# Values of a head pair multiplied by turns, and the levels' score products by turns from the two halves of the rows

## The chip, the cores and the metric

The kernel runs on one core of a Trainium2 chip. The metric is the device time of one execution in microseconds (us), as the median of several runs. TensorE (PE in the profile) multiplies, VectorE (DVE), ScalarE (ACT) and GpSimd (POOL) do the elementwise work, and SyncE (SP) issues the transfers from device memory. Each engine works through its own list of instructions in order. Semaphores make one engine wait for another.

## The reference

Two blocks run one after the other on 256 tokens of width 1024 (272 with the 16 meta tokens in the first block). The first block has two layers, each a mixer and a feed-forward part; the second has gated linear attention (GLA) beside a convolution, then a feed-forward part and a gate. The change touches two places:

```
# first block, first layer: attention, 16 heads, causal
s = jnp.einsum('bqhd,bkhd->bhqk', qb, kb).astype(jnp.float32) * scale
p = jax.nn.softmax(s, axis=-1).astype(vb.dtype)
outs.append(jnp.einsum('bhqk,bkhd->bqhd', p, vb))     # 64 value columns for each head
return o @ w_o
...
# second block: gated linear attention, 4 heads of 64 key and 128 value columns
scores = jnp.einsum('bhtd,bhsd,bhtsd->bhts', qc, kc, decay)
o_intra = jnp.einsum('bhts,bhsv->bhtv', scores, vc)
```

The kernel computes the GLA scores without chunks, level by level: one product of the plain queries and keys for the diagonal, and one for each power of two of the distance.

## The kernel before

All activations lie transposed, with the features on the 128 partitions. A large weight matrix comes in units of some 1 MB through two slots. Each unit is split into a high part (ACT, `high`) and a low part (DVE, POOL, `low`), and every product is three matmuls (lines 436 to 438). The order on each engine is written out by hand.

**Attention.** Tokens are cut into three tiles of 96, 96 and 80. The loop over `s` in the block of TensorE is software-pipelined. At step s, PE does `head_scores(s + 1)`, `head_values(s - 3)` and `head_transposes(s - 2)`. At the steps from 15 on it also does chunks of the output projection (`out_chunks`, six matmuls for each chunk of 128 features). Each fp32 matmul of the program leaves two records in the trace.

- `head_scores(g)` (lines 614 and 616) writes banks 0 to 3 by turns. It waits for the exponentials of head g - 2.
- `head_values(g)` (line 628) multiplies the 64 value columns of head g by its transposed probabilities, with 272, 176 and 80 columns moving. Even heads write partitions 0 to 63 of a bank, odd heads 64 to 127; so the two heads of a pair use two halves of the columns of the PE array. It waits for the copies of the transposed probabilities of head g.
- `head_transposes(g)` (line 644) writes banks 4 and 5.

ACT at its step s does: the copy of the transposed probabilities of head s - 3 (line 1047), the exponentials of head s (line 1056), and at odd s from 5 on the high part of a pair's output (line 1061), which waits for the values of the pair's second head. DVE at its step s does: the row maxima and their negative of head s (lines 1475, 1477), the copies of bank 5 of head s - 3 (lines 1487, 1488), the reciprocals of head s - 1 (line 1495), and at odd s the low part of the pair's output (line 1501), which waits for the high part. POOL scales the probabilities (line 1776) into three buffers. At step 16 ACT first makes the high part of the next weight unit (line 876).

**GLA levels.** `level(l)` (line 764) does eight matmuls with 64 rows of the array each (four for the level `FAR`): first all four from partitions 0 to 63, which write bank 6, then all four from partitions 64 to 127, which write bank 7. There are nine levels, each placed between or within units of the input projections. DVE makes a level's operands (`level_operands`, lines 1557 to 1565), and after its products keeps them by a mask (`level_kept`, line 1579 for all but the last). A level's products wait for its operands and for the masks of the level before; DVE's masks wait for the level's last product.

Of the kernel before, what the change touches and what calls it, by code (L numbers as in the profile page):

```python
# [48 lines left out]
T1 = META + SEQ  # L49
# [4 lines left out]
NH, NOPE, ROPE, VD = 16, 64, 32, 64  # L54
# [8 lines left out]
PTOFF = [0, T1, T1 + 176]  # L63
# [6 lines left out]
FAR, DIAGONAL = 7, 8  # L70
# [117 lines left out]
def program(nc, dram, marks, final):  # L188
    ctx = ExitStack()
    with ctx:  # L190
        def sb(name, shape, dt=F32, stack=None):
            return (stack or ctx).enter_context(nc.sbuf_tensor(name, shape, dt))
# [6 lines left out]
        def done(name, i=None):  # L199


            engine, n, loop = marks.get(name, ("scalar", 1, None))
            stride = marks.get(("stride", engine, loop), 1)
            if final and name not in marks:
                raise KeyError(name)
            if isinstance(i, tuple):
                i, n = i[0], n - i[1] * stride
            return step_sems[engine], n if i is None else i * stride + n
# [42 lines left out]
        V = sb("v_tokens", [96, 3, D], stack=mla)  # L251
# [17 lines left out]
        PT = sb("probs_t", [96, 2, 528], stack=att)  # L269
# [20 lines left out]
        bank = [ctx.enter_context(nc.psum_tensor(f"bank{b}", [P, 512], F32)) for b in range(8)]  # L290
# [125 lines left out]
        def _(pe):  # L416
            S = Steps("tensor", step_sems["tensor"], marks)

            def parts_ready(n, i=None):

                at = n + 1 if i is None else 2 * i + (n + 1)
                pe.wait_ge(high_parts, at)
                pe.wait_ge(low_parts_v, at)
                if pool_share(n):
                    pe.wait_ge(low_parts_g, at)
# [14 lines left out]
            def weights(n, j):  # L440
                return wh[n % 2][:, j * P:(j + 1) * P], wl[n % 2][:, j * P:(j + 1) * P]
# [175 lines left out]
                                            skip_group_check=True)  # L617
                last.then_inc(*S.step(f"scores {g}"))

            def head_values(g):  # L620
                pair, half = g // 2, g % 2
                pe.wait_ge(*done(f"transposed a {g}"))
                pe.wait_ge(*done(f"transposed b {g}"))
                if half == 0 and pair >= 2:
                    pe.wait_ge(*done(f"att out {pair - 2} low"))
                o = bank[6 + pair % 2][64 * half:64 * half + 64, :]
                for c, (k0, nk) in enumerate(QT):
                    last = nc.tensor.matmul(o[:, k0:T1], V[0:nk, c, g * VD:(g + 1) * VD],  # L628
                                            PT[0:nk, g % 2, PTOFF[c]:PTOFF[c] + T1 - k0],
                                            start=c == 0, stop=c == 2)  # L630
                last.then_inc(*S.step(f"values {g}"))

            def head_transposes(g):
                pe.wait_ge(*done(f"probs {g}"))
# [27 lines left out]
            def out_chunks(chunks):  # L662


                n = FIRST_UNIT["wo"]
                for k in chunks:
                    if k == 0:
                        parts_ready(n)
                        pe.wait_ge(*done(f"exp {NH - 2}"))
                    att_ready(k)  # L670
                    for b in range(2):
                        hi, lo = weights(n, k * 2 + b)
                        last = three(bank[BLOCKS[UNITS[n]["first"] + b]["bank"]][:, 0:T1], hi, lo,
                                     uh[:, k, 0:T1], ul[:, k, 0:T1], k == 0, k == DC - 1)
                        if k == DC - 1:
                            last.then_inc(products, 1)

            def att_ready(k):
                pe.wait_ge(*done(f"att out {k} high"))
                pe.wait_ge(*done(f"att out {k} low"))  # L680

            for s in range(2, NH + 3):
                if s + 1 < NH:
                    head_scores(s + 1)
                if s >= 3:
                    head_values(s - 3)
                if s >= NH - 1:
                    out_chunks(((0, 1), (2, 3), (4, 5), (6,))[s - NH + 1])
                if s < NH + 2:
                    head_transposes(s - 2)  # L690
            out_chunks((7,))
# [17 lines left out]
            for half in range(2):  # L709
                for t, (t0, nt_) in enumerate(TT):  # L710
                    b = first + half * len(TT) + t
                    bank_free(b)
                    for g in range(2 * half, 2 * half + 2):
                        out = bank[BLOCKS[b]["bank"]][0:nt_, (g % 2) * 256:(g % 2) * 256 + 256]
                        for k in range(2):
                            if t == 0:
# [4 lines left out]
                            last = nc.tensor.matmul(out, ul[:, 2 * g + k, toks], wh[n % 2][:, at],  # L721
                                                    start=False, stop=k == 1)
# [4 lines left out]
            for c in range(DC):  # L727
                half, g = c // 4, c // 2

                pe.wait_ge(freed["a"], BLOCKS[first + half * len(TT) + len(TT) - 1]["freed"])  # L730
                b = first + 2 * len(TT) + c
                bank_free(b)
                for t, (t0, nt_) in enumerate(TT):
                    last = nc.tensor.matmul(bank[BLOCKS[b]["bank"]][:, t0:T1], pz[0:nt_, t, c * P:(c + 1) * P],  # L734
                                            wm[0:nt_, g, WIN_AT[t]:WIN_AT[t] + T1 - t0],
                                            start=t == 0, stop=t == len(TT) - 1)
# [9 lines left out]
            def level(l):  # L746

                if l == DIAGONAL:
                    pe.wait_ge(freed["v"], BLOCKS[FIRST_BLOCK["gin_k"] + 1]["freed"])
                    pe.wait_ge(*done("gate inputs"))  # L750
                else:
                    pe.wait_ge(*done(f"level {l} q"))
                    pe.wait_ge(*done(f"level {l} k"))
                    pe.wait_ge(*done(f"level {LEVEL_BEFORE[l]} kept 1"))
                qs, ks = (gq, gk) if l == DIAGONAL else (ql, kl)
                for half in range(2):
                    part = slice(64 * half, 64 * half + 64)
                    for pair in range(2):
                        for i in range(2):
                            if l == FAR and i:  # L760
                                continue
                            j = 1 if l == FAR else i
                            o = (pair if l == FAR else pair * 2 + i) * P
                            last = nc.tensor.matmul(bank[6 + half][:, o:o + P],  # L764
                                                    ks[part, pair * SEQ + i * P:pair * SEQ + (i + 1) * P],
                                                    qs[part, pair * SEQ + j * P:pair * SEQ + (j + 1) * P],
                                                    start=True, stop=True)
                last.then_inc(*S.step(f"level {l} scores"))
# [9 lines left out]
            for pair in range(2):  # L778
                last = nc.tensor.matmul(bank[6][:, pair * SEQ:(pair + 1) * SEQ], wgu[:, pair * P:(pair + 1) * P],
                                        glr[0:16, :], start=True, stop=True)  # L780
            last.then_inc(*S.step("gate logits"))

            for v in range(2):
                n = FIRST_UNIT["gin_v"] + v
                parts_ready(n)
                for t in range(2):
                    b = UNITS[n]["first"] + t
                    bank_free(b)
                    out = bank[BLOCKS[b]["bank"]][:, 0:256]
                    for k in range(DC):  # L790
# [3 lines left out]
                        last = nc.tensor.matmul(out, ul[:, k, toks], wh[n % 2][:, at], start=False, stop=k == DC - 1)  # L794
# [24 lines left out]


            level(LEVEL_ORDER[0])
            unit(FIRST_UNIT["gin_g"], T, us)
            level(LEVEL_ORDER[1])
# [1113 lines left out]
```

## Time and profile before

| | |
|---|---|
| median of 3 runs | 966.16 us (965.82 to 967.49) |
| the profiled execution's own time | 969.12 us |
| its span | 967.3 us |
| busy PE, DVE, ACT, POOL | 919.7, 686.3, 513.5, 304.7 us |
| attention loop, values of head 0 to the last output chunk | 80.9 to 128 us |
| GLA levels | 637 to 688 us |

The busy time of an engine is an average over stages with different limits. A row of the timeline gives the start, the length, the engine, the line of the kernel, and in brackets the idle time of the engine just before it with what ended it. Times of one row are from the start of the span.

### The profile page before, as it was taken

What the parts mean: (1) busy time and instruction counts of PE and PEld (TensorE: products, weight loads), DVE (VectorE), ACT (ScalarE), POOL (GpSimd) and SP (SyncE); (2) the same over time, 40 slices, a digit from 0 to 9 for tenths busy, and PEclk for the clock granted to TensorE, in tenths of its full rate; (3) what the DMA queues carried; (4) which work ended last, traced back from release to release, by engine and by line L of the source; (5) the groups of instructions that cost most, each with busy time, mean ns of one, the idle gap of its engine ahead of it and who ended that gap; (6) DMA issues with size and microseconds to landing.
All of it is one profiled execution on the core that took longest, in us unless ns stands there. A gap on an engine that the chain in (4) does not pass through costs nothing.

```text
span 967.3 us, 19946 instructions
## 1 busy us (share of the span) xinstructions
PE 919.7 (95%) x7300; PEld 893.6 (92%) x7300; DVE 686.3 (71%) x1165; ACT 513.5 (53%) x850; POOL 304.7 (31%) x215
## 2 busy tenths in 40 slices
PE   6999998999999998899999899999989999999996
PEld 6997788999998997799999899899989999999995
DVE  7756527999995225599999523879787887885666
ACT  5675655666664335756666444453346444554433
POOL 4107753000004552400000455331226243345643
PEclk9999997999999997899999999899999999999998
DMA  7451032444454451045555445243235555555431
GB/s 255 159 163 44 1 130 88 175 173 173 173 206 155 151 197 67 1 176 193 190 179 206 149 169 198 100 181 131 88 109 192 184 180 179 200 211 201 164 131 44
DMA packets 22145, 146.77 MB, mean 152 GB/s; under 512 B 2752, under 2 KB 5328, under 8 KB 6736
## 3 DMA queue, kind: packets, MB, share of 16 engines
q1 hardware_dynamic: 22096, 146.11, 42.4%
q8 instruction: 32, 0.52, 0.2%
q14 instruction: 17, 0.14, 0.0%
HBM read 143.94 MB, written 1.05 MB: 150 GB/s over the span
## 4 chain that ended last, share of the span: by engine, by line
PE 83%; DVE 11%; ACT 3%; issue 2%; DMA 0%; POOL 0%; SPq 0%; POOLq 0%; DVEq 0%; ACTq 0%
PE bank L436 24%; PE bank L437 23%; PE bank L438 23%; DVE w_low L1227 2%; PE bank L628 2%; PE bank L614 2%; PE bank L506 1%; DVE conv_out L1358 1%; DVE u_low L1236 1%; ACT w_high L876 1%; PE bank L495 1%; PE bank L734 1%; PE bank L644 1%; DVE h L1309 1%; PE bank L764 1%
## 5 line engine op out<-in xcount | busy, mean ns | idle before, releaser
L436 PE MATMUL bank<-u_high,w_high 128*128 128x256 f32 (+2 forms) x1472 | 425.6, 289 | 18.4 <-DVE u_low L1236 16.8
L437 PE MATMUL bank<-u_low,w_high 128*128 128x256 f32 (+2 forms) x1472 | 422.2, 287 | 0.0
L438 PE MATMUL bank<-u_high,w_low 128*128 128x256 f32 (+2 forms) x1472 | 420.8, 286 | 0.0
L1727 POOL TENSOR_TENSOR w_low<-raw,w_high 128x512 fp32r<-128x512 f32 (+1 forms) x73 | 199.8, 2738 | 543.5 <-ACT w_high L876 543.5
L436 PEld LDWEIGHTS bank<-u_high,w_high 128*128 128x128 f32 x1472 | 282.1, 192 | 22.6 <-issue 9.8
L437 PEld LDWEIGHTS bank<-u_low,w_high 128*128 128x128 f32 x1472 | 281.9, 192 | 0.0
L438 PEld LDWEIGHTS bank<-u_high,w_low 128*128 128x128 f32 x1472 | 281.5, 191 | 0.0
L1227 DVE TENSOR_TENSOR w_low<-raw,w_high 128x1024 fp32r<-128x1024 f32 (+5 forms) x119 | 188.8, 1586 | 128.7 <-ACT w_high L876 127.4
L876 ACT ACTIVATE w_high<-raw 128x1024 fp32r<-128x1024 f32 (+5 forms) x120 | 198.0, 1650 | 71.4 <-PE bank L438 61.2
L436 PE MATMUL bank<-x_high,w_high 128*128 128x256 f32 (+1 forms) x608 | 174.9, 288 | 8.0 <-DVE x_low L1335 4.8
L438 PE MATMUL bank<-x_high,w_low 128*128 128x256 f32 (+1 forms) x608 | 174.6, 287 | 0.0
L437 PE MATMUL bank<-x_low,w_high 128*128 128x256 f32 (+1 forms) x608 | 173.9, 286 | 0.0
L436 PEld LDWEIGHTS bank<-x_high,w_high 128*128 128x128 f32 x608 | 116.9, 192 | 9.4 <-ACT conv_out L961 3.4
L437 PEld LDWEIGHTS bank<-x_low,w_high 128*128 128x128 f32 x608 | 116.7, 192 | 0.0
L438 PEld LDWEIGHTS bank<-x_high,w_low 128*128 128x128 f32 x608 | 116.5, 192 | 0.0
L873 ACT ACTIVATE w_high<-raw 128x1024 fp32r<-128x1024 f32 (+1 forms) x66 | 65.8, 996 | 75.8 <-PE bank L438 72.7
L1358 DVE SCALAR_TENSOR_TENSOR conv_out<-conv_in,par,conv_out 128x272 f32<-128x272 f32 (+1 forms) x176 | 85.4, 525 | 6.2 <-ACT conv_out L954 0.7
L1740 POOL TENSOR_TENSOR acc<-acc,sq 128x272 f32<-128x272 f32 (+2 forms) x79 | 63.8, 808 | 76.3 <-ACT sq L892 65.5
L1222 DVE TENSOR_TENSOR w_low<-raw,w_high 128x1024 fp32r<-128x1024 f32 (+1 forms) x66 | 75.4, 1143 | 12.2 <-ACT w_high L873 9.4
L1283 DVE TENSOR_TENSOR conv_in<-bank,r_rows 128x256 f32<-128x256 f32 (+2 forms) x140 | 54.1, 427 | 14.8 <-PE bank L438 9.3
L961 ACT ACTIVATE conv_out<-conv_out 128x272 f32<-128x272 f32 (+1 forms) x44 | 18.8, 426 | 76.6 <-DVE conv_out L1358 76.6
L1236 DVE SCALAR_TENSOR_TENSOR u_low<-h,par,u_high 128x272 fp32r<-128x272 f32 (+3 forms) x56 | 52.6, 957 | 0.9 <-ACT u_high L909 0.9
(194 smaller groups left out, 924.6 us busy)
## 6 DMA issues: line engine op xcount, KB each, us to landing
raw<-w_up_dram SPq DMA_DIRECT2D x66, 1024.0 KB, 4.8
raw<-w_down_dram SPq DMA_DIRECT2D x24, 1408.0 KB, 6.1
raw<-w_gin_c_dram SPq DMA_DIRECT2D x4, 1536.0 KB, 6.3
raw<-w_wo_dram SPq DMA_DIRECT2D x4, 1024.0 KB, 5.0
raw<-w_wout_dram SPq DMA_DIRECT2D x4, 1024.0 KB, 4.8
raw<-w_pgate_dram SPq DMA_DIRECT2D x4, 1024.0 KB, 4.8
raw<-w_gin_v_dram SPq DMA_DIRECT2D x2, 1024.0 KB, 4.9
raw<-w_gin_g_dram SPq DMA_DIRECT2D x2, 1024.0 KB, 4.8
```

Of the source, the lines that this page charges most:

```text
L436: nc.tensor.matmul(out, hi, rhi, start=start, stop=False)
L437: nc.tensor.matmul(out, hi, rlo, start=False, stop=False)
L438: return nc.tensor.matmul(out, lo, rhi, start=False, stop=stop)
L873: nc.scalar.activation(wh[n % 2][:, 0:split], raw[n % 2][:, 0:split], ACT.Copy).then_inc(*S.step(first))
L876: nc.scalar.activation(wh[n % 2][:, split:cols], raw[n % 2][:, split:cols], ACT.Copy).then_inc(high_parts, 1)
L1222: nc.vector.tensor_tensor(wl[n % 2][:, 0:split], raw[n % 2][:, 0:split], wh[n % 2][:, 0:split].bitcast(F32), ALU.subtract).then_inc(*S.step())
L1227: nc.vector.tensor_tensor(wl[n % 2][:, split:cols], raw[n % 2][:, split:cols], wh[n % 2][:, split:cols].bitcast(F32), ALU.subtract).then_i ...
L1236: nc.vector.scalar_tensor_tensor(ul[:, c, 0:T], h[:, c, t0:t0 + T], pcol(gain, c), uh[:, c, 0:T].bitcast(F32), ALU.mult, ALU.subtract)\
L1283: nc.vector.tensor_tensor(out, bank[BLOCKS[b]["bank"]][:, 0:T], rows[:, 0:T], ALU.mult)\
L1358: nc.vector.scalar_tensor_tensor(cv[:, hf, 0:T], ur[:, hf, skip + tap:skip + tap + T], pcol(f"cw{l}", (tap * 2 + hf) * FC + j), cv[:, hf, ...
L1727: nc.gpsimd.tensor_tensor(wl[n % 2][:, at], raw[n % 2][:, at], wh[n % 2][:, at].bitcast(F32), ALU.subtract).then_inc(low_parts_g, pool_cou ...
L1740: nc.gpsimd.tensor_tensor(acc[:, a, 0:T], acc[:, a, 0:T], sq[:, label % 2, 0:T], ALU.add).then_inc(*step)
```

## The change

In attention, `pair_values(pair)` takes the place of `head_values(g)`. It does both heads of a pair, at even steps from 4 on, and goes over the three token tiles, with the two heads by turns within each. It waits for the copies of the pair's second head, so the first head's values come one step later than before. From step 15 on the output chunks now stand ahead of the values. In the levels, the loop over the two halves of the rows becomes the innermost one. No operation is added or taken away, and no other engine's code is changed.

```diff
-            def head_values(g):
-                pair, half = g // 2, g % 2
-                pe.wait_ge(*done(f"transposed a {g}"))
-                pe.wait_ge(*done(f"transposed b {g}"))
-                if half == 0 and pair >= 2:
+            def pair_values(pair):
+                pe.wait_ge(*done(f"transposed a {2 * pair + 1}"))
+                pe.wait_ge(*done(f"transposed b {2 * pair + 1}"))
+                if pair >= 2:
                     pe.wait_ge(*done(f"att out {pair - 2} low"))
-                o = bank[6 + pair % 2][64 * half:64 * half + 64, :]
                 for c, (k0, nk) in enumerate(QT):
-                    last = nc.tensor.matmul(o[:, k0:T1], V[0:nk, c, g * VD:(g + 1) * VD],
-                                            PT[0:nk, g % 2, PTOFF[c]:PTOFF[c] + T1 - k0],
-                                            start=c == 0, stop=c == 2)
-                last.then_inc(*S.step(f"values {g}"))
+                    for half in range(2):
+                        g = 2 * pair + half
+                        last = nc.tensor.matmul(bank[6 + pair % 2][64 * half:64 * half + 64, k0:T1],
+                                                V[0:nk, c, g * VD:(g + 1) * VD],
+                                                PT[0:nk, half, PTOFF[c]:PTOFF[c] + T1 - k0],
+                                                start=c == 0, stop=c == 2)
+                        if c == 2:
+                            last.then_inc(*S.step(f"values {g}"))
...
             for s in range(2, NH + 3):
                 if s + 1 < NH:
                     head_scores(s + 1)
-                if s >= 3:
-                    head_values(s - 3)
                 if s >= NH - 1:
                     out_chunks(((0, 1), (2, 3), (4, 5), (6,))[s - NH + 1])
+                if s >= 4 and s % 2 == 0:
+                    pair_values((s - 4) // 2)
                 if s < NH + 2:
                     head_transposes(s - 2)
...
-                for half in range(2):
-                    part = slice(64 * half, 64 * half + 64)
-                    for pair in range(2):
-                        for i in range(2):
-                            if l == FAR and i:
-                                continue
+                for pair in range(2):
+                    for i in range(2):
+                        if l == FAR and i:
+                            continue
+                        for half in range(2):
+                            part = slice(64 * half, 64 * half + 64)
```

Three places on TensorE show what moves. The first is a step in the middle of the attention loop: the last masking matmul of the scores, one head's values, and the transposes. Before:

```order
L616 MATMUL bank2<-causal_bf16,ident_bf16 80x80
L628 MATMUL bank7<-probs_t,v_tokens 64x272
L628 MATMUL bank7<-probs_t,v_tokens 64x176
L628 MATMUL bank7<-probs_t,v_tokens 64x80
L644 MATMUL bank4<-ident,probs 96x96 x2
L644 MATMUL bank4<-ident,probs 96x80
L644 MATMUL bank5<-ident,probs 96x96
```

Now, at an even step (at odd steps no values stand between the scores and the transposes):

```order
L630 MATMUL bank7<-probs_t,v_tokens 64x272 x2
L630 MATMUL bank7<-probs_t,v_tokens 64x176 x2
L630 MATMUL bank7<-probs_t,v_tokens 64x80 x2
L648 MATMUL bank4<-ident,probs 96x96 x2
L648 MATMUL bank4<-ident,probs 96x80
```

The values of two heads stand in one place, every second step. The second place is the end of the loop (from step 15), where the names with `u_` and `w_` are the output projection. Before, a step's transposes are followed at once by the next head's values:

```order
L644 MATMUL bank5<-ident,probs 80x80
L628 MATMUL bank6<-probs_t,v_tokens 64x272
L628 MATMUL bank6<-probs_t,v_tokens 64x176
L628 MATMUL bank6<-probs_t,v_tokens 64x80
L436 MATMUL bank0<-u_high,w_high1 128x272
L437 MATMUL bank0<-u_low,w_high1 128x272
```

Now the chunks come first, and the values of the pair behind them, ahead of the next transposes:

```order
L436 MATMUL bank2<-u_high,w_high1 128x272
L437 MATMUL bank2<-u_low,w_high1 128x272
L438 MATMUL bank2<-u_high,w_low1 128x272
L630 MATMUL bank6<-probs_t,v_tokens 64x272 x2
L630 MATMUL bank6<-probs_t,v_tokens 64x176 x2
L630 MATMUL bank6<-probs_t,v_tokens 64x80 x2
L648 MATMUL bank4<-ident,probs 96x96 x2
```

The values moved behind the chunks. The third place is a GLA level between two units of the input projection. Before:

```order
L438 MATMUL bank1<-u_high,w_low0 128x256
L764 MATMUL bank6<-gla_q_level,gla_k_level 128x128 x4
L764 MATMUL bank7<-gla_q_level,gla_k_level 128x128 x4
L436 MATMUL bank3<-u_high,w_high1 128x256
L437 MATMUL bank3<-u_low,w_high1 128x256
```

Now:

```order
L438 MATMUL bank1<-u_high,w_low0 128x256
L769 MATMUL bank6<-gla_q_level,gla_k_level 128x128
L769 MATMUL bank7<-gla_q_level,gla_k_level 128x128
L769 MATMUL bank6<-gla_q_level,gla_k_level 128x128
L769 MATMUL bank7<-gla_q_level,gla_k_level 128x128
...
L436 MATMUL bank3<-u_high,w_high1 128x256
```

There are eight such rows (four are shown): the same eight products now change bank, and with it the half of the rows, at each of them.

## Rows read from the trace of the kernel before

**Rows 1.** The page: busy time of each engine, its share and instructions.

```profile
PE 919.7 (95%) x7300; PEld 893.6 (92%) x7300; DVE 686.3 (71%) x1165; ACT 513.5 (53%) x850; POOL 304.7 (31%) x215
```

**Rows 2.** Windows, attention loop: busy us of PE, PEld, DVE, ACT, POOL, clock, DMA.

```profile
78.00:111.80 33.80, 33.72 (x256) 25.80 (x256) 21.09 (x89) 20.27 (x86) 26.44 (x36) 1.00 0.02 8
```

**Rows 3.** Timeline, one pair's round through the engines in the attention loop.

```profile
94.87 1.11 PE L628 MATMUL bank<-probs_t,v_tokens 96*64 96x272 f32 x6
...
95.91 0.67 PE L644 MATMUL bank<-ident,probs 96*96 96x96 f32 x6
...
96.61 0.39 ACT L1047 ACTIVATE probs_t<-bank 96x272 f32<-96x272 f32 x1 [0.96 <-PE bank L644]
...
96.91 0.33 ACT L1056 ACTIVATE probs<-bank,neg_max 96x96 f32<-96x96 f32 x1
...
98.08 0.40 ACT L1061 ACTIVATE u_high<-bank 128x272 fp32r<-128x272 f32 x1
98.51 0.44 DVE L1501 TENSOR_TENSOR u_low<-bank,u_high 128x272 fp32r<-128x272 f32 x1 [1.33 <-ACT u_high L1061]
...
98.87 0.86 DVE L1475 TENSOR_REDUCE row_max<-bank 96x1 f32<-96x96 f32 x3
...
100.10 0.23 DVE L1488 COPY probs_t<-bank 80x80 f32<-80x80 f32 x1
...
100.47 1.11 PE L628 MATMUL bank<-probs_t,v_tokens 96*64 96x272 f32 x6
```

**Rows 4.** Timeline, around the values of heads 0 and 1.

```profile
81.49 0.20 ACT L1056 ACTIVATION_READ_ACCUMULATOR probs<-bank,neg_max 80x1 f32 x1
...
82.41 0.35 PE L614 MATMUL bank<-k_heads,q_heads 96*96 96x96 f32 x2
...
83.66 0.67 PE L628 MATMUL bank<-probs_t,v_tokens 96*64 96x272 f32 x2
```

**Rows 5.** Timeline, end of the attention loop.

```profile
111.79 1.11 PE L628 MATMUL bank<-probs_t,v_tokens 96*64 96x272 f32 x6
...
112.83 0.67 PE L644 MATMUL bank<-ident,probs 96*96 96x96 f32 x6
...
115.14 0.39 PE L436 MATMUL bank<-u_high,w_high 128*128 128x272 f32 x1
...
115.29 1.93 ACT L876 ACTIVATE w_high<-raw 128x2048 fp32r<-128x2048 f32 x1
...
116.75 0.63 PE L644 MATMUL bank<-ident,probs 96*96 96x96 f32 x6
...
118.08 3.63 POOL L1776 TENSOR_SCALAR probs<-probs,row_inv 96x96 f32<-96x96 f32 x3 [1.67 <-DVE row_inv L1495]
...
125.85 1.08 PE L628 MATMUL bank<-probs_t,v_tokens 96*64 96x272 f32 x6 [0.67 <-DVE probs_t L1488]
...
127.99 0.36 PE L436 MATMUL bank<-u_high,w_high 128*128 128x272 f32 x1
```

**Rows 6.** Timeline of PE in one GLA level, the whole and narrow windows of it.

```profile
644.58 1.71 PE L764 MATMUL bank<-gla_q_level,gla_k_level 64*128 64x128 f32 x16
...
644.79 0.49 PE L764 MATMUL bank<-gla_q_level,gla_k_level 64*128 64x128 f32 x3
...
645.13 0.60 PE L764 MATMUL bank<-gla_q_level,gla_k_level 64*128 64x128 f32 x6
...
646.02 0.27 PE L764 MATMUL bank<-gla_q_level,gla_k_level 64*128 64x128 f32 x1
646.22 0.39 PE L436 MATMUL bank<-u_high,w_high 128*128 128x256 f32 x1
```

**Rows 7.** Timeline of DVE, the three masks that wait for a level's products.

```profile
646.33 1.38 DVE L1579 COPY_PREDICATED gla_s_diag<-level_masks,bank 128x512 f32<-128x512 int32 x2 [1.21 <-PE bank L764]
...
657.35 1.40 DVE L1579 COPY_PREDICATED gla_s_diag<-level_masks,bank 128x512 f32<-128x512 int32 x2 [0.36 <-PE bank L764]
...
669.44 1.40 DVE L1579 COPY_PREDICATED gla_s_diag<-level_masks,bank 128x512 f32<-128x512 int32 x2 [0.82 <-PE bank L764]
```

## The prediction

> **What bounds the kernel now.** I read the page first: PE is busy for 919.7 of 967.3 us [rows 1], so what shortens PE's list can shorten the whole, but only in a stretch where nothing else ends last. So I looked at the two stretches that the change touches. In the attention loop the window shows PE busy for 33.72 of 33.80 us at the full clock, with POOL at 26.44, DVE at 21.09 and ACT at 20.27 [rows 2]. That looks like a stretch that only PE bounds. The timeline says more. I follow one pair's round from engine to engine [rows 3]. The values of a pair's second head start at 94.87 and last 1.04 until the transposes at 95.91, which end at 96.58. ACT copies (96.61), does its exponentials (96.91), then the pair's high part (98.08). DVE, which has sat idle for 1.33 us, makes the low part (98.51) and only then the next row maxima (98.87) and the copy of bank 5, which ends at 100.33. The next second head's values need that copy, and start at 100.47. The round is 5.60 us, and PE's own work of two steps is 5.60 us too. Two limits stand side by side, and the change shortens only one of them.
>
> In the GLA levels I read PE's and DVE's timelines. One level is 16 records from 644.58 to 646.22, 1.64 us [rows 6]. DVE waits for a level's products three times in all, by 1.21, 0.36 and 0.82 us [rows 7]; after all other levels the products are long there when DVE comes to mask them.
>
> **Do two halves of the array run side by side?** For halves of the rows the level's own rows answer. Three records of one half take 0.49 us and one takes 0.27, so one half steps at 0.11 us [rows 6]. Around the change of halves six records start and end within 0.60 us [rows 6], where a single line of them would have four (0.27 + 3 x 0.11). So the second half's records run beside the last ones of the first. By turns, eight records of each half run beside each other from the start. The second half begins about one step late (0.11), the first record is 0.10 longer, then seven steps of 0.11, and 0.20 from the last start to the next unit as now [rows 6]: 0.11 + 0.10 + 0.77 + 0.20 = 1.18 to 1.20 instead of 1.64, so 0.44 us less for each level. The bounds are 0 (no more overlap than now) and 0.55 (no late start).
>
> For halves of the columns (the values) no row of this trace has two such matmuls next to each other. Let d be what a pair's burst takes over one head's 1.04. If they run beside each other as the row halves do, d is one late start, 0.11. If they don't, d is a second head's streaming: 0.11 us for a record of 128 columns [rows 6] makes 0.92 for 2 x (272 + 176 + 80) columns. So d lies between 0 and 0.92, and I take 0.11, because two disjoint halves of one array are what the level rows show.
>
> The Trainium skill, TensorE: Matmul & The Clock Gate, section on packing small matmuls, would have matmuls strictly in order of start and end, and weight loads pulled beside running matmuls only where the row groups differ. The two heads of a pair use the same rows, so by that rule they would take about the serial time, which is the first rival below. The same section gives three column tiles a measured gain of 2.38 times, and by its span model a tile more costs some 4 ns, which would make d almost nothing. The six records within 0.60 us speak against its strict order of starts.
>
> **Attention, step by step.** (a) At step 3 the values of head 0 go. The scores of head 5 (82.41) could come some 1.1 us earlier (the burst of 1.04 and about 0.1 for the change into it, as the first record of a level shows [rows 6]), but they wait for the exponentials of head 3, which end at 81.69 [rows 4]. So they start at about 81.75, take 1.25 as now (82.41 to 83.66), and the first pair starts at 83.0 instead of 83.66: -0.65. (b) From here each pair starts one round after the other. The round through ACT and DVE has the pair's burst in it and nothing else of what changes, so it becomes 5.60 + d. PE's own work falls to 5.60 - 1.04 - 0.1 + d, about 4.6: the former overlap of two limits ends, and PE gets an idle gap of about 1 us ahead of each pair's values. Five rounds lie between the first pair and the one at 111.79: +5d. This is where most of the freed PE time goes. (c) The end of the loop. Now each head's values wait out the copy of the transposes just ahead (0.67 at 125.85 [rows 5]), four times. Afterwards the chunks (1.6 us for two, 115.14 to 116.75 [rows 5]) stand in that place and hide it. From the transposes at 112.83 by PE's own list the next pair could start at 112.83 + 0.50 + 1.5 + 0.47 + 1.6 = 116.9. But ACT makes a weight unit's high part from 115.29 to 117.22 and copies only then (0.39), so it starts at 117.7. Then 1.04 + d for it, 0.5 for transposes, 1.5 for chunks: transposes of head 15 at 120.75. Their probabilities come from POOL, whose row of 3.63 us starts at 118.08 [rows 5]; it is released by a copy that now comes some 1.8 us earlier, so it ends by 119.9 and stays hidden. The last pair starts 1.3 later, at 122.1, and the last chunk follows as now 2.14 after it (125.85 to 127.99 [rows 5]), at 124.25 instead of 127.99: -3.7, with 3d for three bursts on the way. In sum the loop ends -4.35 + 8d later, at d = 0.11 it is -3.5 us. What follows moves with it as one piece.
>
> **Levels.** The diagonal and the first level are each 0.44 shorter, and DVE's wait of 1.21 gives back 0.88. From there DVE is the one that is late, and level 1's products start when its operands are there. The wait of 0.36 ahead of the third mask goes altogether, as PE is 0.44 further ahead. Then three levels on PE, and the wait of 0.82 goes altogether too. 0.88 + 0.36 + 0.82 = 2.06 us. After 669.44 DVE no longer waits for a level, so the rest of the levels' PE time (9 x 0.44 less that) buys nothing. The bounds are 0 and 2.39, the sum of the three waits.
>
> **Sum.** -3.5 - 2.05 = -5.55 us. The profiled execution's own time is 969.12, span 967.3; it lies 0.3% over the median, and I take the difference off the median: 966.16 - 5.55 = 960.6.
>
> **Rivals.**
> - *The columns' halves run one after the other* (d = 0.92). For it: no row shows otherwise. Against it: the row halves do run beside each other. Attention +3.0, levels -2.05: +0.95, 967.1.
> - *Each change of half costs a drain.* This is the one on the other side. Entering a level costs 0.10 on its first record [rows 6]; if each of five turns within a pair's burst cost that as well as the serial time, d = 1.4, attention +6.9, in all +4.8, 971.0. It decides from d = 0.8 on, where loss and gain are even. Against it: the change of halves within a level costs nothing now. The Trainium skill, TensorEngine Tiling (Array Packing), key properties, has a drain for a change of the tiling mode, not of the tile; the trace agrees for halves of the rows.
> - *PE alone bounds the loop*, and my round through ACT and DVE has slack. Then each of five rounds falls by 1.14 - d = 1.03 instead of growing by d: 5.7 us more gained, 954.9. Against it: DVE's idle 1.33 us sits in the round, and its copy ends just 0.14 ahead of the values.
> - *Part of the gain is swallowed*: d near 0.3 and half of the levels' 2.05. -4.35 + 2.4 - 1.0 = -3, 963.2. DVE is nearly full around the levels, which speaks for it.
>
> **Numbers.** Mine 0.66, serial columns 0.15, a drain at each turn 0.05, PE alone 0.06, partly swallowed 0.08. A difference under 0.2% (1.9 us) is about what a measurement of this kernel can't tell from no change. Mine, PE alone and partly swallowed are faster: 0.80, less a little for their edges; serial columns is mostly within 0.2%; its edge and the drain are slower. Mine alone lies within 959 to 962.6 (d from 0.05 to 0.2, levels 1.5 to 2.4). The range reaches down half a microsecond and up to the serial case: 958.4 to 967.2.
>
> **What would show it.** After the change a pair's values should be one burst of 12 records in about 1.15 us at eight places, with starts in between closer than 0.07 us; about 2 us would mean serial. The pairs' bursts should stand 5.7 us apart, with PE idle about 1 us ahead of each, ended by DVE's copy (line 1488's operation); 4.6 us apart would make PE alone the bound. The last chunk should start 3 to 4 us earlier. A level should take 1.2 us, and the three waits of DVE should be near nothing but for 0.3 at the first. The prediction is wrong above all if d is far from 0.11, since it counts eight times.

## The result and the profile after

The changed kernel takes 961.3 us in the median of four runs (960.62 to 961.49), beside 966.83 for the kernel before in the same comparison (four runs, 965.82 to 968.22). The ratio is 0.9935, with a 95% interval of 0.9922 to 0.9949: 5.5 us faster. The forecast was 960.6, a gain of 5.55, in a range of 958.4 to 967.2.

The page answers to [rows 1]: PE's busy time fell by 12.4 us, the median time by 5.5. (The two profiled executions lie 7.7 us apart, 967.3 against 959.6 in their spans, since that of the kernel before was a long one.)

```profile
span 959.6 us, 19938 instructions
PE 907.3 (95%) x7300; PEld 883.8 (92%) x7300; DVE 685.2 (71%) x1165; ACT 512.4 (53%) x850; POOL 304.8 (32%) x215
```

The window over the attention loop (busy us of PE, PEld, DVE, ACT, POOL with their instructions, then clock and DMA) shows where the rest stayed.

```profile
78.00:111.00 33.00, 28.48 (x251) 22.17 (x251) 20.54 (x91) 19.72 (x86) 26.28 (x37) 1.00 0.01 3
```

In [rows 2] PE had 0.08 us idle in 33.80; now it has 4.5 idle in 33.00, at the same clock. The timeline of one round, engine by engine (start, duration, what; in brackets the idle time ahead and what ended it), says why. It answers to [rows 3].

```profile
94.08 1.12 PE L630 MATMUL bank<-probs_t,v_tokens 96*64 96x272 f32 x12 [0.79 <-ACT probs L1061]
95.12 0.67 PE L648 MATMUL bank<-ident,probs 96*96 96x96 f32 x6
...
97.73 0.44 DVE L1506 TENSOR_TENSOR u_low<-bank,u_high 128x272 fp32r<-128x272 f32 x1 [1.33 <-ACT u_high L1066]
98.08 0.86 DVE L1480 TENSOR_REDUCE row_max<-bank 96x1 f32<-96x96 f32 x3
...
99.31 0.23 DVE L1493 COPY probs_t<-bank 80x80 f32<-80x80 f32 x1
...
99.64 1.12 PE L630 MATMUL bank<-probs_t,v_tokens 96*64 96x272 f32 x12 [0.79 <-ACT probs L1061]
```

The twelve records of a pair now take 1.04 us until the transposes (94.08 to 95.12), as long as the six of one head before. The next pair starts 5.56 later, where [rows 3] had 5.60. The wait ahead of it is put down to ACT's exponentials, but the values don't wait for those in the program: what they wait for and what ends last is DVE's copy, at 99.54, 0.10 ahead. The chain of waits, which follows back from one step to what released it, shows the same round: values, transposes, exponentials, high part, low part, row maxima. The three rows set apart behind it are from an earlier round, where the chain names the copy itself.

```profile
94.08 1.12 PE bank L630 x12
95.19 0.61 PE bank L648 x6
95.87 0.25 issue
96.12 1.28 ACT probs L1061 x6
97.41 0.29 ACT u_high L1066
97.73 0.44 DVE u_low L1506
98.17 0.78 DVE row_max L1480 x3
```

```profile
87.00 0.78 DVE row_max L1480 x3
88.14 0.23 DVE probs_t L1493
88.51 1.12 PE bank L630 x12
```

The end of the loop on PE, for [rows 5]:

```profile
82.90 1.12 PE L630 MATMUL bank<-probs_t,v_tokens 96*64 96x272 f32 x12
...
110.92 1.12 PE L630 MATMUL bank<-probs_t,v_tokens 96*64 96x272 f32 x12 [0.79 <-ACT probs L1061]
...
116.67 1.12 PE L630 MATMUL bank<-probs_t,v_tokens 96*64 96x272 f32 x12 [0.47 <-ACT probs_t L1052]
...
121.12 1.12 PE L630 MATMUL bank<-probs_t,v_tokens 96*64 96x272 f32 x12
123.33 0.36 PE L436 MATMUL bank<-u_high,w_high 128*128 128x272 f32 x1 [1.09 <-DVE u_low L1506]
```

The last chunk starts at 123.33 instead of 127.99, 4.66 earlier. Only 0.87 of it was there at 110.92, which answers to 111.79; the other 3.8 came from the last two pairs, which take the time of one head each and whose copies now go on beside the chunks. The two traces are already 0.15 apart at the first score product (66.43 and 66.28), so that 4.5 of the 4.66 belong to the loop.

The levels on PE, for [rows 6]:

```profile
638.09 1.16 PE L769 MATMUL bank<-gla_q_level,gla_k_level 64*128 64x128 f32 x16
639.18 0.38 PE L436 MATMUL bank<-u_high,w_high 128*128 128x256 f32 x1
...
648.39 1.79 PE L769 MATMUL bank<-gla_q_level,gla_k_level 64*128 64x128 f32 x16 [1.98 <-DVE gla_k_level L1564]
650.11 0.58 PE L436 MATMUL bank<-u_high,w_high 128*128 128x256 f32 x1
...
655.43 1.16 PE L769 MATMUL bank<-gla_q_level,gla_k_level 64*128 64x128 f32 x16
...
660.93 1.16 PE L769 MATMUL bank<-gla_q_level,gla_k_level 64*128 64x128 f32 x16
```

DVE's masks that still wait, for [rows 7]:

```profile
639.30 1.40 DVE L1584 COPY_PREDICATED gla_s_diag<-level_masks,bank 128x512 f32<-128x512 int32 x2 [0.53 <-PE bank L769]
...
650.21 1.38 DVE L1584 COPY_PREDICATED gla_s_diag<-level_masks,bank 128x512 f32<-128x512 int32 x2 [0.47 <-PE bank L769]
...
662.13 1.40 DVE L1584 COPY_PREDICATED gla_s_diag<-level_masks,bank 128x512 f32<-128x512 int32 x2 [0.34 <-PE bank L769]
```

A level takes 1.09 us until the next unit (638.09 to 639.18), where [rows 6] had 1.64: 0.55 less. But the one at 648.39 takes 1.72, and the next one stands 7.04 behind it, where the one after that stands 5.50. The windows say what it was (the clock is the column with 1.00, 0.66, 0.50):

```profile
646.00:648.40 2.40, 0.42 (x6) 0.25 (x4) 2.37 (x6) 0.00 (x0) 0.00 (x0) 1.00 0.47 102
648.40:649.50 1.10, 1.10 (x13) 1.10 (x15) 1.07 (x4) 0.39 (x2) 0.00 (x0) 0.66 0.94 402
649.50:650.50 1.00, 1.00 (x9) 0.78 (x7) 0.54 (x2) 1.00 (x3) 0.00 (x0) 0.50 0.98 418
650.50:652.00 1.50, 1.50 (x9) 1.50 (x9) 1.47 (x4) 1.50 (x1) 0.00 (x0) 0.50 0.74 311
652.00:654.00 2.00, 2.00 (x18) 2.00 (x18) 1.97 (x4) 0.49 (x1) 1.43 (x1) 0.96 0.00 0
```

PE had been idle for 1.98 us, waiting for DVE's operands, and during the level its granted clock fell from 2.4 to 1.2 GHz, until about 652. So DVE's wait at 650.21 did not go away. From the GLA stage's start to its end the trace is only 1.2 us shorter than before.

### The profile page after: what moved, and what is told of

Same layout as the page of the kernel before. It is cut to its first block, busy times and chain, and to the rows that moved or that the text cites. A ratio compares the mean times of both kernels' runs of the same rounds, so it can differ in the third digit from the quotient of the medians.

```text
span 959.6 us, 19938 instructions
## 1 busy us (share of the span) xinstructions
PE 907.3 (95%) x7300; PEld 883.8 (92%) x7300; DVE 685.2 (71%) x1165; ACT 512.4 (53%) x850; POOL 304.8 (32%) x215
## 3 DMA queue, kind: packets, MB, share of 16 engines
HBM read 143.94 MB, written 1.05 MB: 151 GB/s over the span
## 4 chain that ended last, share of the span: by engine, by line
PE 81%; DVE 12%; ACT 5%; issue 2%; DMA 0%; POOL 0%; SPq 0%; POOLq 0%; DVEq 0%; ACTq 0%
PE bank L436 24%; PE bank L437 23%; PE bank L438 23%; DVE w_low L1232 2%; ACT w_high L881 2%; DVE conv_out L1363 1%; DVE u_low L1241 1%; PE bank L506 1%; ACT probs L1061 1%; PE bank L495 1%; PE bank L738 1%; PE bank L630 1%; DVE h L1314 1%; DVE bank L1306 1%; PE bank L490 1%
```

## Experiments

All times are medians of the whole kernel with the ratio to the kernel before on the same chip. Where I give a stage, it is read from the trace, as the distance of two matmuls of TensorE that stand ahead of and behind it: 117.37 us before and 112.85 after for the attention with what lies around it, 82.36 and 81.14 for the levels.

**Values alone.** The kernel before with the new `pair_values` and its place in the loop, the levels as before:

```
-                if s >= 3:
-                    head_values(s - 3)
                 if s >= NH - 1:
                     out_chunks(((0, 1), (2, 3), (4, 5), (6,))[s - NH + 1])
+                if s >= 4 and s % 2 == 0:
+                    pair_values((s - 4) // 2)
```

> The attention half of the change alone (pairs' values by turns, chunks first), the levels as before. My theory (column halves run beside each other, the round through ScalarE and VectorE stays at 5.6 us, the end of the loop gives 3.7 to 4.7): 3.5 to 4.7 us under the kernel before, ratio 0.995 to 0.9965, last chunk of the loop near 123.3 us, a pair's burst near 1.05 us. Rival (the levels brought most of the gain): under 2 us.

It took 963.66 us (961.01 to 964.59), ratio 0.9962 (0.9948 to 0.9976): 3.1 less in the medians, just under what was expected, and 3.7 by the ratio. The pairs stand 5.56 apart and the attention stage is 4.55 shorter in the trace; the levels' stage is within 0.1 of before.

**Levels alone.** The kernel before with the levels' loops turned:

```
-                for half in range(2):
-                    part = slice(64 * half, 64 * half + 64)
-                    for pair in range(2):
-                        for i in range(2):
+                for pair in range(2):
+                    for i in range(2):
...
+                        for half in range(2):
+                            part = slice(64 * half, 64 * half + 64)
```

> The level half of the change alone, attention as before. My theory: every level about 0.45 to 0.55 us shorter on TensorE, VectorE's three waits of 1.21, 0.36 and 0.82 us shrink, 1.2 to 2.05 us under the kernel before (ratio 0.9979 to 0.9988), and 1.0 us less than that if the clock falls in one level as in the changed kernel. Rival (all nine levels' TensorE time reaches the end): 4 us or more.

It took 966.33 us (964.42 to 968.1), ratio 0.9993 (0.9984 to 1.0002): by the time alone no gain can be told from nothing. In the trace the stage is 1.27 us shorter, and the same level is slow after the same idle time:

```profile
646.99 1.16 PE L765 MATMUL bank<-gla_q_level,gla_k_level 64*128 64x128 f32 x16
653.16 1.78 PE L765 MATMUL bank<-gla_q_level,gla_k_level 64*128 64x128 f32 x16 [1.98 <-DVE gla_k_level L1560]
660.19 1.16 PE L765 MATMUL bank<-gla_q_level,gla_k_level 64*128 64x128 f32 x16
```

So the half clock there comes with the levels' change, and not from what the attention stage does.

**The pair's heads one behind the other.** The changed kernel, with two loops swapped:

```
-                for c, (k0, nk) in enumerate(QT):
-                    for half in range(2):
+                for half in range(2):
+                    for c, (k0, nk) in enumerate(QT):
```

> The changed kernel, but a pair's twelve records go head by head instead of by turns; place, waits and levels as in the changed kernel. My theory: the second head overlaps only the last records of the first, a burst of 1.4 to 1.6 us instead of 1.05, counted eight times: 2.8 to 4.4 us over the changed kernel. Rival (the place and the merging bring the gain, not the turns): within 1 us of the changed kernel, burst about 1.05. Rival (no overlap at all head by head): burst about 1.95, 7 us over the changed kernel.

It took 963.87 us (962.28 to 966.48), ratio 0.9966 (0.9954 to 0.9978), which is 2.6 over the changed kernel in the medians and 3.0 by the ratios. A burst and its round on PE:

```profile
96.32 1.60 PE L630 MATMUL bank<-probs_t,v_tokens 96*64 96x272 f32 x12 [0.79 <-ACT probs L1061]
97.85 0.67 PE L648 MATMUL bank<-ident,probs 96*96 96x96 f32 x6
...
102.36 1.60 PE L630 MATMUL bank<-probs_t,v_tokens 96*64 96x272 f32 x12 [0.79 <-ACT probs L1061]
```

The burst takes 1.53 us instead of 1.04, and the round grows from 5.56 to 6.04 by just that, while PE's idle time ahead of it stays 0.79. Over seven rounds that is 3.4 us (first to last burst 41.63 instead of 38.22 us). This is the test of the term 8d: what a burst costs more, every round costs more, though PE has idle time in it. In the trace the whole loop is 3.9 us longer, so the time shows less of it than the trace. The run also shows that placing both heads together isn't enough; the order by turns is worth 0.49 a pair.

**Both heads in one half of the columns.** The changed kernel, where from the third pair on both heads write partitions 0 to 63, of two different banks, so that both use the same 64 columns of the array. The attention's output is another one by that.

```
-                    pe.wait_ge(*done(f"att out {pair - 2} low"))
+                    pe.wait_ge(*done(f"att out {pair - 1} low"))
...
-                        last = nc.tensor.matmul(bank[6 + pair % 2][64 * half:64 * half + 64, k0:T1],
+                        b, p0 = (6 + pair % 2, 64 * half) if pair < 2 else (6 + (pair + half) % 2, 0)
+                        last = nc.tensor.matmul(bank[b][p0:p0 + 64, k0:T1],
```

> The changed kernel, but from the third pair on both heads write partitions 0 to 63 of two different banks, so that they use the same half of the array's columns; order, waits and counts stay, the output of the attention is another one. My theory (the two halves of the columns make the overlap, not the order of the rows in the program): burst 1.95 us for these six pairs instead of 1.05, pairs 6.4 to 6.5 us apart, 5 to 5.5 us over the changed kernel. Rival (the order or the two banks make it): burst stays near 1.05 and the time too.

It took 967.08 us (965.4 to 968.77), ratio 0.9999 (0.9988 to 1.0009).

```profile
100.33 1.98 PE L631 MATMUL bank<-probs_t,v_tokens 96*64 96x272 f32 x12 [0.79 <-ACT probs L1062]
102.24 0.67 PE L649 MATMUL bank<-ident,probs 96*96 96x96 f32 x6
```

With the same six matmuls (twelve records) in the same order, the burst is 1.91 us instead of 1.04. So the halves of the columns are what lets two heads share the time of one, 0.87 us of it. The round grows to 6.42, by the same 0.86, with PE's idle time unchanged at 0.79. This is the forecast's serial rival, built for six of the eight pairs: d = 0.87 measured against 0.92 worked out, and 0.5 us below its kernel before where the rival was put 0.95 above; the two pairs that still stand side by side are 1.7 us of that. Against the changed kernel, each beside its own runs of before (−0.5 and −6.3), it loses 5.8 us.

**The chunks first, heads apart.** The kernel before, with the output chunks ahead of the values and nothing else:

```
-                if s >= 3:
-                    head_values(s - 3)
                 if s >= NH - 1:
                     out_chunks(((0, 1), (2, 3), (4, 5), (6,))[s - NH + 1])
+                if s >= 3:
+                    head_values(s - 3)
```

> The kernel before with one edit: from step 15 on the output chunks stand ahead of the values, which stay one head per step. My theory: the four waits of 0.65 us for the copies go, the last chunk waits about 1 us more, and the wait behind the weight unit's high part stays: 1.2 to 2.2 us under the kernel before, nothing changed in the rounds before step 15. Rival (the end of the loop is bound by other engines): within 0.5 us of the kernel before.

It took 966.21 us (963.86 to 968.59), ratio 0.9994 (0.9983 to 1.0005), not to be told from no change by the time: 0.55 less in the medians where 1.2 to 2.2 was expected. So the gain is shown by the trace alone. There the last values start at 124.36 and none of the last four waits any more; the attention stage is 2.1 us shorter. The idle times that it removes are 0.62 to 0.67, four of them. So the chunks' place brings about 2 of the attention's 4.5 us. The other 2.4 are what is left of two things that work against each other. As an estimate from the run above, 8 x 0.87 = 7 us come from the heads side by side, and the rest of that goes where both heads' products now stand in one burst inside the round.

**DVE's low part one step later.** The round was said to go through DVE, where the low part of a pair's output (line 1506) stands ahead of the row maxima and the copy that the next pair waits for. Here that low part stands one step later on DVE, in the changed kernel:

```
-                if s >= 5 and s % 2 == 1:
-                    pair = (s - 5) // 2
+                late = s >= 6 and s % 2 == 0 and s <= NH
+                if late or s >= NH + 1 and s % 2 == 1:
+                    pair = (s - 6) // 2 if late else (s - 5) // 2
                     dve.wait_ge(*done(f"att out {pair} high"))
```

> The changed kernel with VectorE's low part of a pair's output moved out of the round: one step later, behind the next copy and reciprocals (pairs 0 to 5). My theory (the round through ScalarE and VectorE holds the pairs 5.6 us apart, while TensorE's own work is 4.5 to 4.7): pairs 4.6 to 4.8 us apart, 4 to 5 us under the changed kernel. Rival (TensorE or GpSimd bounds the loop): pairs stay 5.5 us or more apart and the time stays within 1 us of the changed kernel.

It took 958.38 us (957.08 to 959.87), ratio 0.9913 (0.9899 to 0.9927).

```profile
92.38 1.12 PE L630 MATMUL bank<-probs_t,v_tokens 96*64 96x272 f32 x12
...
97.08 1.12 PE L630 MATMUL bank<-probs_t,v_tokens 96*64 96x272 f32 x12
```

The window over the loop:

```profile
78.00:108.00 30.00, 29.66 (x268) 23.00 (x267) 22.13 (x93) 20.43 (x89) 27.79 (x39) 1.00 0.01 5
```

The pairs now stand 4.70 us apart, nothing is idle ahead of them, and PE is busy for 29.66 of 30.00 us. Five rounds take 23.48 us (82.99 to 106.47) instead of 28.02, and the last chunk starts at 118.87 instead of 123.33. PE's idle time in the round was real, and the place of one subtraction on DVE was what kept it.

The loop is thus 4.5 us shorter, but the whole kernel is not. On this chip the changed kernel took 960.97 (see below), so the gain is 2.6 us in the medians, where 4 to 5 was expected, and 2.9 in the spans of the two traces. The difference lies behind the loop, where PE's list is the same. Two stretches in which the clock is halved are longer in this trace, the first two rows, than in that of the changed kernel on the same chip, the last two:

```profile
140.60:150.80 10.20, 7.05 (x29) 6.68 (x30) 8.28 (x21) 7.05 (x15) 4.41 (x7) 0.50 0.17 70
355.60:369.20 13.60, 9.15 (x38) 7.77 (x38) 11.49 (x26) 8.70 (x18) 5.69 (x8) 0.50 0.01 1
```

```profile
147.00:154.00 7.00, 5.03 (x21) 4.77 (x22) 6.74 (x18) 4.93 (x12) 3.83 (x5) 0.51 0.00 0
362.20:372.40 10.20, 7.83 (x32) 6.50 (x33) 10.17 (x22) 6.11 (x15) 5.37 (x7) 0.50 0.01 2
```

At each of them the lead over the changed kernel falls by 0.6 us. Whether the earlier end of the loop causes that isn't shown.

**The same move in the kernel before.** The same edit, heads one at a time.

> The same move in the kernel before, whose TensorE work for a pair of steps is 5.60 us by itself. My theory: the two limits stood side by side, so the round alone gives nothing: heads stay 2.80 us apart, time within 1 us of the kernel before. Rival (the round alone was the limit): heads under 2.7 us apart, 2 us or more faster.

It took 966.7 us (966.04 to 968.41), ratio 0.9999 (0.999 to 1.0008). The heads stand 2.80 apart, as before. So the move is worth nothing while PE's own list is as long as the round, and 4.5 us of the loop (2.6 of the whole) once it is shorter. The two limits that stood side by side in [rows 3] are thereby each shown by itself.

**DVE's weight unit behind the second mask.** The changed kernel, with one low part of a weight unit moved behind the operands of level 2, so that PE doesn't wait 1.98 us for them:

```
             level_operands(1)
-            low(n + 6)
             level_kept(1)
             level_operands(2)
+            low(n + 6)
```

> The changed kernel with VectorE's low part of one weight unit (2304 columns, 2.5 us) moved behind the operands of the level of distance 4, so that this level's products no longer wait for it. My theory (the levels' gain of 2.05 was cut to 1.2 because TensorE sat idle for 1.98 us there and its granted clock then was halved for 3.4 us): this level starts 1.9 us earlier, the idle time moves behind it and is 1.5 us or less, the level's records step at 0.11 us and not at 0.21, and the stage is 0.5 to 1.5 us shorter. Rival (the clock does not hang on that wait): the half clock stays somewhere in the stage and the stage is within 0.3 us of the changed kernel.

It took 960.42 us (958.48 to 961.96), ratio 0.9933 (0.992 to 0.9946).

**The changed kernel again**, on the same chip beside it.

> The changed kernel itself on this chip, as the measure for the other three. Every theory expects 0.9922 to 0.9949 of the kernel before, the pairs 5.57 us apart and the level stage 1.2 us shorter than before.

It took 960.97 us (960.17 to 962.64), ratio 0.9939 (0.9927 to 0.9951). Its pairs stand 5.56 apart again, and its levels' stage is that of the first trace to 0.1 us, the slow level included. So the time can't tell the unit's move from none (0.55 us in the medians, inside both ranges). In the trace with the unit moved, the level is at the full clock and the levels' stage 1.36 us shorter than in the changed kernel:

```profile
645.04 1.16 PE L769 MATMUL bank<-gla_q_level,gla_k_level 64*128 64x128 f32 x16
647.93 0.36 PE L436 MATMUL bank<-u_high,w_high 128*128 128x256 f32 x1 [1.74 <-issue]
...
670.69 1.51 PE L769 MATMUL bank<-gla_q_level,gla_k_level 64*128 64x128 f32 x16 [1.80 <-DVE gla_k_level L1564]
```

PE is still idle once for 1.74 (1.5 or less was expected), now behind the level, without a fall of the clock. But the level at 670.69, behind another idle time of 1.80, is slow here, as the rival had it that the half clock stays somewhere in the stage:

```profile
671.00:674.00 3.00, 3.00 (x24) 2.77 (x21) 3.00 (x7) 2.58 (x3) 0.00 (x0) 0.56 0.03 8
```

In the changed kernel the same level (673.80, behind 1.82 us) ran at the full clock.

**Both moves together** in the changed kernel:

> The changed kernel with both moves on VectorE (the low part of a pair's output one step later, the low part of one weight unit behind the operands of the level of distance 4). My theory (the two gains lie in different stages and add): loop end 4.4 us earlier than in the changed kernel, level stage 1.0 to 1.4 us shorter, 5 to 6 us under the changed kernel, ratio to the kernel before 0.989 to 0.991. Rival (the half clock turns up elsewhere and eats the second gain): same as the first move alone, 0.991 to 0.992.

It took 957.44 us (956.85 to 958.8), ratio 0.9899 (0.9882 to 0.9916), 10.1 us less than before. It is the fastest of all kernels here. Beside the changed kernel's 6.3 on its chip that is 3.8 us more, where 5 to 6 was expected. Its pairs stand 4.70 apart, its levels all run at the full clock, and the levels' stage is 1.8 us shorter than in the changed kernel. From the first score product (68.07 here) the loop is 4.5 us shorter than in the changed kernel. Beside the first move alone (0.9913) the second adds 0.0014, less than the intervals can part.

## Why the prediction was right, point by point

**The columns' halves.** That two heads in two halves of the columns run beside each other was right, and no row of the trace of before had shown it. Moved into one half, the same six matmuls take 1.91 us instead of 1.04. The term of the sum that was mis-sized is d: it was put at "one late start, 0.11" from the change of row halves, and a burst took 1.04 to 1.05, as long as one head's, so d is 0.01 at most. The first two records of a burst start 7 ns apart in the trace. With eight times 0.10 this is 0.8 us more gained. The late start could have been seen to be small in the trace of before. In the level of [rows 6] the second half's first record (a long one of 0.37 us, as the first of a half is) starts 6 ns behind one of the first half's, and ahead of three more of them. The Trainium skill, TensorE: Matmul & The Clock Gate, section on packing small matmuls, gives some 4 ns for each further tile in its span model; here the first records of the two heads start 7 ns apart and the later pairs of records 36 or 37, and the burst is at most 0.01 us longer than one head's, so the trace agrees in size. Its rule in the same section that loads overlap only where the row groups differ would, as the forecast read it, have made these bursts serial; the measured 1.04 against 1.91 says otherwise, for halves of the columns with the same rows, in float32.

**The first pair (a).** 83.0 was forecast, 82.90 measured. Such times from the start of the span carry what happened ahead of the loop (with both moves the first pair starts at 84.69). From the first score product to the first pair it is 17.23 us before and 16.61 or 16.62 in all eight traces in which a pair's values stand together: 0.61 less, with 0.65 forecast.

**The round (b).** It was right that the round through ACT and DVE keeps its length (5.60 + d forecast, 5.56 to 5.61 measured but for one of 5.72), that PE gets an idle time of about 1 us (0.79), and that the gain in the middle of the loop is thus small: only 0.87 us had been gained by the pair at 110.92. Three runs show it from three sides: a longer burst lengthens each round by as much, a shorter way through DVE brings 4.5 us of the loop, and the same shorter way in the kernel before brings nothing. The rival in which PE alone bounds the loop was wrong for this kernel, but with DVE's low part moved it comes true: it had priced five rounds at 1.03 less each than before, and they are 0.93 less each (23.48 instead of 28.13 us).

**The end of the loop (c).** The last pair was forecast at 122.1 and starts at 121.12, the last chunk at 124.25 and starts at 123.33. Both forecast times leave out the 0.65 and the 8d; with them the loop's end was put at −3.5. Counted from the first score product it is −4.5 (−4.66 from the start of the span). Of the 1.0 us between them 8d is 0.8, and five rounds that are a little under 5.60 are 0.1; from the pair at 110.92 to the last chunk it is 12.41 us, where the steps gave 124.25 − 111.79 = 12.46. The part of the mechanism, chunks that cover the copies, was shown by itself: 2.1 us.

**The levels.** The size of one level was too small: 0.44 forecast and 0.55 measured, the bound that was given for "no late start". The gain of the stage was too large: 2.05 against 1.2. DVE's three masks wait 0.53, 0.47 and 0.34 us, where 0.3, 0 and 0 were forecast. The first of them stands 4.19 behind the mask ahead of it instead of 5.13, a gain of 0.94 with 0.88 forecast. What failed is the step "The wait of 0.36 ahead of the third mask goes altogether, as PE is 0.44 further ahead", and with it the same for the wait of 0.82. PE is further ahead, so it waits longer for DVE's operands, 1.98 us in one piece where it had waited 0.99 and 0.64 at two levels, and the clock fell in the level behind it. That level and the units behind it cost 7.04 − 5.50 = 1.54 us. DVE's second wait hangs on it: with the unit moved it is gone, in two traces. The third does not: it is still 0.26 and 0.27 there. With the unit moved, the stage gains 2.6 us in all in the trace, and 3.0 with both moves, more than the bound of 2.39, since DVE's own order is then another one. Why the clock falls behind one such idle time and not behind another isn't settled. At the level of 648.39 it fell behind 1.97 or 1.98 us in all six traces that have the levels' change and not the unit's move. Behind the later idle time of 1.80 to 1.82 it fell in one trace and stayed in seven, and behind 1.74 it stayed in two.

**The sum.** Two terms were mis-sized in opposite directions, attention by −1.0 and levels by +0.85, so the sum of −5.55 meets the measured 5.5 partly by luck. The rival of a gain partly swallowed was right about the levels and wrong about d. A part of what a single trace shows comes from neither stage: between the attention and the levels the changed kernel's trace gains 1.4 us more on that of before, in two pieces. The first falls where the half clock lasts from 149.8 to 160.0 before and from 147.0 to 153.8 after, the second where it lasts from 364.8 to 378.5 and from 362.0 to 372.3. Values alone and levels alone, 3.1 and 0.4 in the medians and 4.6 and 1.3 in the traces, show that scatter too.

## What to carry to other kernels

Here matmuls that use half of the array's columns ran two in the time of one only with the two halves' instructions by turns in the program. With one head behind the other they kept 0.38 of the 0.87 us and lost 0.49. A level in halves of the rows went from 1.64 to 1.09 us by the same turn. When an engine is busy all the time and its work equals the length of a round through other engines, shortening it uncovers the round; look for the instruction in that round whose result is wanted last, here a subtraction that only a later pair and the output chunks wait for, and move it behind those that are wanted at once (0.9 us a round here). Then read the whole kernel's time too: of 4.5 us of the loop 2.6 arrived at its end. Where TensorE is made faster ahead of a wait, the wait grows, and what follows it can run at half the clock.

## What was not expected of the hardware

- Two float32 matmuls with the same 96 rows and different 64 columns start 7 ns apart at the head of a burst, and the pair takes no longer than one: six matmuls (twelve records) in 1.04 us, against 1.91 in one half.
- Head behind head in different halves, part of them overlapped even so (1.53 us instead of 1.91), and the second head's first record started at 96.81, ahead of three of the first head's that stand before it in the program (96.95, 97.10 and 97.18).
- Behind 1.98 us of idle TensorE the granted clock was 1.2 GHz up to about 652 in the changed kernel, and so it was at the same level in the five other traces with that idle time, while an idle time of 1.82 in the same kernel left it at 2.4 GHz.
